# Two decoder layers' attention: pairs of heads across key groups, values in groups, scores at alternate ends of a step

## The chip, the cores and the metric

The kernel runs on one core of a Trainium2 chip. The metric is the device time of one launch in microseconds (us), as the median of a few runs. Smaller is better. All data is 32-bit floating point at input and output.

## The reference, cut to what matters

The reference is one block of a first kind (a mixer, cross attention and a feed-forward net) and then two layers of a second kind, over 512 tokens of width 1024. Only the attention of the two layers of the second kind concerns the change:

```
q, k, v, u, ug, ga, gb = split(rmsnorm(x) @ w_in)          # 16 query heads, 2 key heads, 64 wide
q, k = rope(rmsnorm(q)), rope(rmsnorm(k))
# query block of 128 tokens i sees key blocks i-1 and i; window 128; head n uses key head n // 8
s = q k^T / 8, masked;  m = max(max(s), sink)
p = exp(s - m) / (sum(exp(s - m)) + exp(sink - m));   a = p v
c = conv_branch(u, ug) @ w_conv_out                        # 31 taps, layer norm, silu
x = x + (sigmoid(ga) * a + sigmoid(gb) * c) @ w_out
x = x + feed_forward(x)
```

## The kernel before, in words

Every engine has its own program, written out by hand; semaphores order them, and each engine runs its program strictly in order. Weights come in a stream of units of 1 MB through three slots. ScalarE splits each into a high part (`split_hi`), VectorE takes the rest as a low part (`split_lo`), and each product of a 128x128 weight tile with 512 tokens is three matmuls, high by high, high by low, low by high (lines 415 to 417). Such a triple is called a chunk below.

Inside a layer, the attention is cut into 32 jobs. Job j is one block of 128 queries and one pair of heads. The blocks come in the order 1, 2, 3, 0; a job of block 0 (the last eight, 24 to 31) has one key block instead of two. The stage is a hand-written loop of 36 steps. In step t TensorE does, in this order: the scores of job t (`scores`, line 2110: two heads, each in its own 64 rows of the array), the turning of the probabilities of job t-3 (`turn`, line 2120: up to four 128x128 transposes into one bank), some chunks of other products of the layer that need no attention (`fill_chunks`, counts in `FILL_AT`), and the values of job t-4 (`values`, line 2133: two heads, each in its own 64 columns of the array). Here S(j), T(j) and V(j) name these, and fill(t) the chunks of step t. One fp32 matmul is two records in the trace.

Between them, for each job: VectorE adds the mask and takes the maximum (`softmax`, line 2415, one instruction a head) and, after that of the next job, the reciprocal of the sums (line 2419). ScalarE takes the exponential of both heads (`exps`, line 2260) and copies the turned probabilities to `lprobT` (`copy_turned`, line 2267; there is one bank, so T(j) waits for the copy of j-1). GpSimd scales the probabilities (`scaled`, line 2590). VectorE multiplies the values by the gate (`gated`, line 2427). The three engines do other work of the layer in the same loop: layer norm of the convolution (squares at line 2289, a square root at line 2292, silu at line 2296), gates, weight splits, and from step 29 the merge. A merge of part k is a sum on GpSimd (`merged`, line 2595), its high part on ScalarE (`merged_hi`, line 2273) and its low part on VectorE (`merged_lo`, line 2440). In steps 32 to 35 TensorE takes one part k each, 0 to 3, into the output products (`out_products`, three chunks), and after the loop parts 4 to 7. Each waits for `merged_lo(k)`.

The keys of the two heads of a pair are in one 64-row half of the array; a swapped copy `lkx` of the keys, made by ScalarE, serves the other half.

Of the kernel before, what the change touches and what calls it, by code (L numbers as in the profile page):

```python
# [100 lines left out]
def build(nc, w, x, mem, pos, pack, tables, cmask, w2, wg, rope2, out):  # L101
    ctx = ExitStack()
    with ctx:
# [104 lines left out]
        lkx = place("lkx", [P, T], F32, a)  # L208
# [16 lines left out]
        cos_q, perm_q = place("cos_q", [P, T], F32, a), place("perm_q", [P, P], F32, a)  # L225
        b = [a[0]]
        lsq = place("lsq", [P, 2, T + 4], F32, b)
        lcos = place("lcos", [P, 2, T + 4], F32, b)
        lwide = place("lwide", [P, QB * P], F32, b)
        b = [a[0]]  # L230
        lprob = place("lprob", [P, 4, 2, 2 * P + 2], F32, b)
        lprobT = place("lprobT", [P, 2, 4, P], F32, b)
# [1613 lines left out]
        def cross_dve(dve):  # L1846
# [84 lines left out]
        q_sq, q_ss, q_std, q_inv, q_row, q_n, q_rot, q_cos, q_sin, q_rope, l_kx = (sem("l_" + n) for n in (  # L1931
            "q_sq", "q_ss", "q_std", "q_inv", "q_row", "q_n", "q_rot", "q_cos", "q_sin", "q_rope", "kx"))
# [8 lines left out]
        LJ = QB * 8  # L1941

# [6 lines left out]
        LAG_T, LAG_V = 3, 4  # L1949

# [15 lines left out]
        MERGE_HI_AT, MERGE_LO_AT = 29, 30  # L1966
# [31 lines left out]
        def layer_pe(pe, L):  # L1998
# [99 lines left out]
            def scores(j):  # L2098
                i, tile, g = block_of(j), j % 8, j % 8 // 4
                if j == 0:  # L2100
                    pe.wait_ge(l_kx, L * 2 + 2)
                    pe.wait_ge(l_g, L * 16 + 10)
# [5 lines left out]
                for e in range(2):  # L2108
                    keys = key_rows(lq[:, 8, :], lkx[:, :], e, g)[:, k0:(i + 1) * P]
# [13 lines left out]
            def values(j):  # L2123
                i, g = block_of(j), j % 8 // 4
                first = 1 if i == 0 else 0
                pe.wait_ge(A["turned_copied"], L * LJ + j + 1)
                if j == 0:
                    pe.wait_ge(q_rope, L * 9 + 9)
                else:
                    pe.wait_ge(A["gated"], L * LJ + j)  # L2130
                for c in range(first, 2):
                    for e in range(2):
                        mm = pe.matmul(bank[HD * e:HD * e + HD, 6, 0:P], lv[:, i - 1 + c, g * HD:(g + 1) * HD],  # L2133
                                       lprobT[:, j % 2, 2 * e + c, :], start=(c == first), stop=(c == 1))
# [12 lines left out]
            for t in range(STEPS):  # L2147
                if t < LJ:
                    scores(t)
                if t == 1:  # L2150
                    rotate(8)
                if 0 <= t - LAG_T < LJ:
# [11 lines left out]
                if 0 <= t - LAG_V < LJ:  # L2164
                    values(t - LAG_V)
# [6 lines left out]
                if t == AT_SS:  # L2172
                    pe.wait_ge(ln_add, L * 3 + 3)
                    pe.wait_ge(l_gs, L * 16 + 12)
                    column_sums(pe, bank[:, 7, 0:QB], conv_squares(0)).then_inc(cstat_done, 1)

# [10 lines left out]
        def layer_act(act, L):  # L2187
# [21 lines left out]
            for n in range(V_FILL):  # L2209
# [39 lines left out]
                if n == ROPE_UNITS[0] + 2:  # L2249
                    act.wait_ge(q_rope, L * 9 + 1)  # L2250
# [508 lines left out]
```

## Time and profile before

| what | value |
|---|---|
| median of 3 runs | 2247.55 us (2246.56 to 2248.97) |
| span of the profiled execution | 2246.4 us |
| median less that span | 1.15 us |
| TensorE busy | 2224.9 us, 99% |
| VectorE, ScalarE, GpSimd busy | 1245.1, 885.6, 280.7 us |
| attention stage of layer 0, S(0) to the end of V(31) | 1033.15 to 1154.85 us |

A record of TensorE says when a matmul starts and ends, and the ends are modelled, so its busy share says little about waits. What an operation takes of TensorE's time is read from the start of its first record to the start of the next operation's. Idle time in brackets names the engine that released the instruction. Both layers run the same program; the stage of layer 1 shows the same steps as that of layer 0 to a few hundredths of a microsecond.

### The profile page before, as it was taken

What the parts mean: (1) busy time and instruction counts of PE and PEld (TensorE: products, weight loads), DVE (VectorE), ACT (ScalarE), POOL (GpSimd) and SP (SyncE); (2) the same over time, 40 slices, a digit from 0 to 9 for tenths busy, and PEclk for the clock granted to TensorE, in tenths of its full rate; (3) what the DMA queues carried; (4) which work ended last, traced back from release to release, by engine and by line L of the source; (5) the groups of instructions that cost most, each with busy time, mean ns of one, the idle gap of its engine ahead of it and who ended that gap; (6) DMA issues with size and microseconds to landing.
All of it is one profiled execution on the core that took longest, in us unless ns stands there. A gap on an engine that the chain in (4) does not pass through costs nothing.

```text
span 2246.4 us, 29245 instructions
## 1 busy us (share of the span) xinstructions
PE 2224.9 (99%) x11388; PEld 1821.7 (81%) x11388; DVE 1245.1 (55%) x1836; ACT 885.6 (39%) x1363; POOL 280.7 (12%) x273
## 2 busy tenths in 40 slices
PE   9999999999999999999999999999999999999999
PEld 7877888898888888886778888888887668888887
DVE  6467656445444225999664444333889664544422
ACT  5545454354333225234744333222323753433321
POOL 3000032011000001014331000001003442000000
PEclk9999999999999999999999999999999999999999
DMA  6221033122222231321122222222221112322222
GB/s 223 100 76 57 20 121 126 55 72 99 103 102 93 94 113 69 113 75 57 56 77 81 107 93 93 100 106 105 104 84 57 39 66 85 113 102 104 94 101 86
DMA packets 30484, 203.19 MB, mean 90 GB/s; under 512 B 3504, under 2 KB 4144, under 8 KB 6704
## 3 DMA queue, kind: packets, MB, share of 16 engines
q1 hardware_dynamic: 29088, 197.34, 24.4%
q10 hardware_dynamic: 1296, 4.46, 0.5%
q8 instruction: 69, 1.13, 0.2%
q14 instruction: 31, 0.25, 0.0%
HBM read 199.69 MB, written 2.10 MB: 90 GB/s over the span
## 4 chain that ended last, share of the span: by engine, by line
PE 93%; DVE 3%; POOL 1%; ACT 1%; issue 1%; DMA 0%; ACTq 0%; DVEq 0%; POOLq 0%
PE bank L415 26%; PE bank L417 26%; PE bank L416 26%; PE bank L2110 1%; PE bank L1002 1%; PE bank L2120 1%; PE bank L2133 1%; PE bank L973 1%; PE bank L2028 1%; POOL acc L324 1%; PE bank L990 1%; PE bank L2010 1%; PE bank L1593 1%; PE bank L1570 1%; PE bank L515 1%
## 5 line engine op out<-in xcount | busy, mean ns | idle before, releaser
L415 PE MATMUL bank<-x_hi,w_hi 128*128 128x512 f32 (+1 forms) x2032 | 789.9, 389 | 5.9 <-DVE x_lo L1766 2.3
L417 PE MATMUL bank<-x_hi,w_lo 128*128 128x512 f32 (+1 forms) x2032 | 775.0, 381 | 0.0
L416 PE MATMUL bank<-x_lo,w_hi 128*128 128x512 f32 (+1 forms) x2032 | 774.1, 381 | 0.0
L301 DVE TENSOR_TENSOR w_lo<-w_raw,w_hi 128x2048 fp32r<-128x2048 f32 x167 | 386.2, 2313 | 412.3 <-ACT w_hi L297 412.3
L297 ACT ACTIVATE w_hi<-w_raw 128x2048 fp32r<-128x2048 f32 x167 | 319.7, 1916 | 585.8 <-PE bank L417 583.9
L415 PEld LDWEIGHTS bank<-x_hi,w_hi 128*128 128x128 f32 x2032 | 382.1, 188 | 83.6 <-issue 6.8
L417 PEld LDWEIGHTS bank<-x_hi,w_lo 128*128 128x128 f32 x2032 | 381.9, 188 | 74.9
L416 PEld LDWEIGHTS bank<-x_lo,w_hi 128*128 128x128 f32 x2032 | 382.4, 188 | 72.7 <-issue 2.9
L415 PE MATMUL bank<-f_hi,w_hi 128*128 128x512 f32 (+1 forms) x572 | 213.3, 373 | 0.0
L416 PE MATMUL bank<-f_lo,w_hi 128*128 128x512 f32 (+1 forms) x572 | 213.2, 373 | 0.0
L417 PE MATMUL bank<-f_hi,w_lo 128*128 128x512 f32 (+1 forms) x572 | 213.2, 373 | 0.0
L2345 DVE SCALAR_TENSOR_TENSOR cy<-la,gains,cy 128x512 f32<-128x512 f32 x240 | 173.9, 794 | 0.0
L563 DVE TENSOR_TENSOR bank<-bank,rbc 128x512 f32<-128x512 f32 x66 | 46.0, 697 | 167.6 <-PE bank L417 159.6
L415 PEld LDWEIGHTS bank<-f_hi,w_hi 128*128 128x128 f32 x572 | 107.7, 188 | 19.0
L416 PEld LDWEIGHTS bank<-f_lo,w_hi 128*128 128x128 f32 x572 | 107.7, 188 | 18.9
L417 PEld LDWEIGHTS bank<-f_hi,w_lo 128*128 128x128 f32 x572 | 107.7, 188 | 18.7
L324 POOL TENSOR_TENSOR acc<-acc,sq 128x512 f32<-128x512 f32 (+1 forms) x48 | 77.6, 1618 | 144.2 <-ACT sq L308 140.4
L552 ACT ACTIVATE f_hi<-bank 128x512 f32 x66 | 39.6, 599 | 115.5 <-DVE bank L569 115.5
L571 DVE TENSOR_TENSOR f_lo<-bank,f_hi 128x512 f32 x66 | 45.7, 692 | 58.4 <-ACT f_hi L552 58.4
L2590 POOL TENSOR_TENSOR lprob<-lprob,small 128x512 f32<-128x512 f32 (+1 forms) x64 | 61.9, 967 | 123.6 <-DVE small L2419 77.8
L2260 ACT ACTIVATE lprob<-lprob,small 128x257 f32<-128x257 f32 (+1 forms) x128 | 60.5, 475 | 31.5 <-DVE small L2415 30.9
L324 POOL TENSOR_TENSOR acc<-sq 128x512 f32<-128x512 f32 (+1 forms) x8 | 14.4, 1801 | 442.8 <-ACT sq L308 442.8
(355 smaller groups left out, 2637.2 us busy)
## 6 DMA issues: line engine op xcount, KB each, us to landing
w_raw<-w_d SPq DMA_DIRECT2D x184, 1024.0 KB, 4.8
out_d<-h SPq DMA_DIRECT2D x8, 256.0 KB, 6.6
h<-x_d ACTq DMA_DIRECT2D x3, 512.0 KB, 9.2
tab<-rope_d ACTq DMA_DIRECT2D x2, 640.0 KB, 3.9
memT<-mem_d ACTq DMA_DIRECT2D x1, 1024.0 KB, 4.8
w_raw<-w_d SPq DMA_DIRECT2D x2, 256.0 KB, 4.1
h<-x_d ACTq DMA_DIRECT2D x2, 256.0 KB, 5.8
w_raw<-w_d SPq DMA_DIRECT2D x1, 512.0 KB, 6.6
```

The costliest lines, as they stand in the source:

```text
L297: act.activation(w_hi[:, u.slot, :], w_raw[:, u.slot, :], ACT.Copy).then_inc(hi_ready, 1)
L301: dve.tensor_tensor(w_lo[:, u.slot, :], w_raw[:, u.slot, :], w_hi[:, u.slot, :], ALU.subtract).then_inc(lo_ready, 1)
L324: pool.tensor_tensor(acc[:, 0:width], sq[:, 0, 0:width] if k == 1 else acc[:, 0:width], sq[:, k % 2, 0:width], ALU.add).then_inc(acc_ready, 1)
L415: pe.matmul(dst, wh[:, k, cols], hi[:, kx_, at:at + width], start=start, stop=False)
L416: pe.matmul(dst, wh[:, k, cols], lo[:, kx_, at:at + width], start=False, stop=False)
L417: return pe.matmul(dst, wl[:, k, cols], hi[:, kx_, at:at + width], start=False, stop=stop)
L552: act.activation(pick(f_hi, j, i), up, ACT.Copy).then_inc(f_hi_done, 1)
L563: dve.tensor_tensor(g, g, rbc[:, :], ALU.mult).then_inc(gu_scaled, 1)
L571: dve.tensor_tensor(pick(f_lo, j, i), up, pick(f_hi, j, i), ALU.subtract).then_inc(f_lo_done, 1)
L2260: act.activation(row, row, ACT.Exp, bias=asm(j, 0, e), scale=-1.0, accum_out=asm(j, 4, e)).then_inc(A["exp"], 1)
L2345: dve.scalar_tensor_tensor(out=cy[:, m, :], in0=src, scalar=wt, in1=cy[:, m, :], op0=ALU.mult, op1=ALU.add).then_inc(l_tap, 1)
L2590: pool.tensor_tensor(row, row, asm(j, 12).unsqueeze(2).to_broadcast([P, 2, 2 * P - c0]), ALU.mult).then_inc(A["scaled"], 1)
```

## The change

Heads n and n+8 form a pair, one of each key head, so that each half of the array finds its own key head where the rotated keys lie; `lkx` and its two copies go. The weights' columns are put in that order ahead of the launch. The turned probabilities are kept for four jobs (`lprobT`), and the values of four jobs of one block, or of two in block 0, are one product of up to 512 columns (`GROUPS`, `values(n)`), with one `gated` for the group; they stand in steps 7, 11, 15, 19, 23, 27, 29, 31, 33 and 35. In an even step the scores stand last and not first, and with them that step's `softmax` on VectorE and `exps` on ScalarE: an even job's scores and the next odd job's are then neighbours. The merge starts in step 31 instead of 29 (GpSimd, ScalarE) or 30 (VectorE).

```diff
         a = [scope]
         lq = place("lq", [P, 9, T], F32, a)
-        lkx = place("lkx", [P, T], F32, a)
...
-        cos_q, perm_q = place("cos_q", [P, T], F32, a), place("perm_q", [P, P], F32, a)
+        perm_q = place("perm_q", [P, P], F32, a)
...
+        turned_at = b[0]
         lwide = place("lwide", [P, QB * P], F32, b)
+        cos_q = place("cos_q", [P, T], F32, b)
         b = [a[0]]
         lprob = place("lprob", [P, 4, 2, 2 * P + 2], F32, b)
-        lprobT = place("lprobT", [P, 2, 4, P], F32, b)
+        assert b[0] == turned_at
+        lprobT = place("lprobT", [P, 2, 2, 4, P], F32, b)
...
                                         "pv", "gated")}
         sink_in = sem("a_sink_in")
         LJ = QB * 8
+        GROUPS = [range(j, j + 4) for j in range(0, 24, 4)] + [range(j, j + 2) for j in range(24, LJ, 2)]
+        NG = len(GROUPS)
+        GROUP_OF = [n for n, js in enumerate(GROUPS) for _ in js]
...
         V_FILL = 14
         ROPE_UNITS = range(10, 15)
         LAG_T, LAG_V = 3, 4
+        VALUES_AT = {js[-1] + LAG_V: n for n, js in enumerate(GROUPS)}
+
+        def group_cols(n):
+
+            js = GROUPS[n]
+            return slice(js[0] % 4, js[-1] % 4 + 1)
         FILL_BANK = (5, 7, 5, 7, 7, 5) + (7, 5) * 4
...
         CENTRE_AT, SQ_AT, NORM_AT, LO_AT = ({t: (0, 1), t + 1: (2, 3)} for t in (3, 3, AT_ROWS, AT_LO))
         L_SPLIT_AT = {3: (16, 0), 4: (16, 1), 5: (17, 0), 8: (17, 1), 16: (18, 0), 17: (18, 1), 18: (19, 0), 21: (19, 1),
                       25: (20, 0), 28: (20, 1), 33: (21, 0), 34: (21, 1)}
-        MERGE_HI_AT, MERGE_LO_AT = 29, 30
+        MERGE_HI_AT, MERGE_LO_AT = 31, 31
         OUT_AT = {32: (0,), 33: (1,), 34: (2,), 35: (3,)}
         STEPS = LJ + LAG_V
...
                 if j < 8:
                     pe.wait_ge(q_rope, L * 9 + j + 2)
                     pe.wait_ge(A["max"], (L * LJ + j - 1) * 2)
                 c0, k0 = (P, 0) if i == 0 else (0, (i - 1) * P)
                 for e in range(2):
-                    keys = key_rows(lq[:, 8, :], lkx[:, :], e, g)[:, k0:(i + 1) * P]
+                    keys = lq[HD * e:HD * e + HD, 8, k0:(i + 1) * P]
                     pe.matmul(bank[:, score_bank(j) + e, c0:2 * P], lq[HD * e:HD * e + HD, tile, i * P:(i + 1) * P], keys,
                               start=True, stop=True).then_inc(A["scores"], 1)
...
                         mm = pe.transpose(bank[:, 4, (2 * e + c) * P:(2 * e + c + 1) * P], lprob[:, prob_at(j), e, c * P:(c + 1) * P], ident[:, :])
                 mm.then_inc(A["turned"], 1)
-            def values(j):
-                i, g = block_of(j), j % 8 // 4
+            def values(n):
+                js, cols = GROUPS[n], group_cols(n)
+                i = block_of(js[0])
                 first = 1 if i == 0 else 0
-                pe.wait_ge(A["turned_copied"], L * LJ + j + 1)
-                if j == 0:
+                pe.wait_ge(A["turned_copied"], L * LJ + js[-1] + 1)
+                if n == 0:
                     pe.wait_ge(q_rope, L * 9 + 9)
                 else:
-                    pe.wait_ge(A["gated"], L * LJ + j)
+                    pe.wait_ge(A["gated"], L * NG + n)
                 for c in range(first, 2):
                     for e in range(2):
-                        mm = pe.matmul(bank[HD * e:HD * e + HD, 6, 0:P], lv[:, i - 1 + c, g * HD:(g + 1) * HD],
-                                       lprobT[:, j % 2, 2 * e + c, :], start=(c == first), stop=(c == 1))
+                        mm = pe.matmul(bank[HD * e:HD * e + HD, 6, cols.start * P:cols.stop * P], lv[:, i - 1 + c, e * HD:(e + 1) * HD],
+                                       lprobT[:, e, c, cols, :].rearrange("p m t -> p (m t)"), start=(c == first), stop=(c == 1))
                 mm.then_inc(A["pv"], 1)
...
             fill_chunks(FILL_FIRST)
             for t in range(STEPS):
-                if t < LJ:
+                if t < LJ and t % 2:
                     scores(t)
                 if t == 1:
                     rotate(8)
+                if t in VALUES_AT:
+                    values(VALUES_AT[t])
                 if 0 <= t - LAG_T < LJ:
                     turn(t - LAG_T)
                 fill_chunks(FILL_AT.get(t, 0))
...
                         pe.wait_ge(lo_ready, Unit(base + V_OUT + 1, L).n + 1)
                         pe.wait_ge(co_ready, L * 8 + 8)
                     out_products(((1, 1), (0, 0), (0, 1)), OUT_AT[t])
...
                     pe.wait_ge(ln_add, L * 3 + 3)
                     pe.wait_ge(l_gs, L * 16 + 12)
                     column_sums(pe, bank[:, 7, 0:QB], conv_squares(0)).then_inc(cstat_done, 1)
+                if t < LJ and t % 2 == 0:
+                    scores(t)
             out_products(((1, 1), (0, 0), (0, 1)), range(4, 8)).then_inc(unit_done, 1)
             out_products(((1, 0),), range(8)).then_inc(unit_done, 1)
...
-                    act.activation(lkx[HD:P, :], lq[0:HD, 8, :], ACT.Copy).then_inc(l_kx, 1)
             def exps(j):
...
             def copy_turned(j):
                 act.wait_ge(A["turned"], L * LJ + j + 1)
-                if j >= 2:
-                    act.wait_ge(A["pv"], L * LJ + j - 1)
+                if j == 0:
+                    act.wait_ge(q_rope, L * 9 + 9)
+                if j >= 4:
+                    act.wait_ge(A["pv"], L * NG + GROUP_OF[j - 4] + 1)
                 first = 1 if block_of(j) == 0 else 0
-                act.activation(lprobT[:, j % 2, :, :].rearrange("p (e c) t -> p e c t", e=2)[:, :, first:, :],
+                act.activation(lprobT[:, :, first:, j % 4, :],
                                bank[:, 4, :].rearrange("p (e c t) -> p e c t", e=2, c=2)[:, :, first:, :], ACT.Copy)\
                    .then_inc(A["turned_copied"], 1)
...
             for t in range(STEPS):
                 if 0 <= t - LAG_T < LJ:
                     copy_turned(t - LAG_T)
-                if t < LJ:
+                if t < LJ and t % 2:
                     exps(t)
                 for f in FILL_END.get(t - 1, ()):
                     if f < 6:
                     for m in range(4):
                         act.wait_ge(ln_y, L * 4 + m + 1)
                         act.activation(c_hi[:, m, :], cy[:, m, :], ACT.Copy).then_inc(ln_hi, 1)
+                if t < LJ and t % 2 == 0:
+                    exps(t)
                 if MERGE_HI_AT <= t:
                     merged_hi(t - MERGE_HI_AT)
...
                     dve.wait_ge(A["exp"], (L * LJ + o + 1) * 2)
                     dve.reciprocal(asm(o, 12), asm(o, 4)).then_inc(A["rec"], 1)
-            def gated(j):
-                i, tile = block_of(j), j % 8
-                dst = sga[:, tile, i * P:(i + 1) * P]
-                dve.wait_ge(A["pv"], L * LJ + j + 1)
-                if j == 0:
+            def gated(n):
+                js, cols = GROUPS[n], group_cols(n)
+                i, tile = block_of(js[0]), js[0] % 8
+                dst = sga[:, tile:tile + len(js), i * P:(i + 1) * P]
+                dve.wait_ge(A["pv"], L * NG + n + 1)
+                if n == 0:
                     dve.wait_ge(l_g, L * 16 + 8)
-                dve.scalar_tensor_tensor(out=dst, in0=dst, scalar=1.0, in1=bank[:, 6, 0:P], op0=ALU.add, op1=ALU.mult).then_inc(A["gated"], 1)
+                pv = bank[:, 6, cols.start * P:cols.stop * P].rearrange("p (m t) -> p m t", t=P)
+                dve.scalar_tensor_tensor(out=dst, in0=dst, scalar=1.0, in1=pv, op0=ALU.add, op1=ALU.mult).then_inc(A["gated"], 1)
             def conv_gated(k):
...
             taps(FIRST_TAPS)
             for t in range(STEPS):
-                softmax(t, t - 1)
-                if 0 <= t - LAG_V < LJ:
-                    gated(t - LAG_V)
+                if t % 2 or t >= LJ:
+                    softmax(t, t - 1)
+                if t in VALUES_AT:
+                    gated(VALUES_AT[t])
                 if t == STEPS - 1:
-                    dve.wait_ge(A["gated"], L * LJ + LJ)
+                    dve.wait_ge(A["gated"], L * NG + NG)
...
                 for m in LO_AT.get(t, ()):
                     dve.wait_ge(ln_hi, L * 4 + m + 1)
                     dve.tensor_tensor(c_lo[:, m, :], cy[:, m, :], c_hi[:, m, :], ALU.subtract).then_inc(ln_lo, 1)
+                if t % 2 == 0 and t < LJ:
+                    softmax(t, t - 1)
             for k in range(STEPS - MERGE_LO_AT, DT):
                 merged_lo(k)
...
                 pool.tensor_tensor(row, row, asm(j, 12).unsqueeze(2).to_broadcast([P, 2, 2 * P - c0]), ALU.mult).then_inc(A["scaled"], 1)
             def merged(L, k):
-                pool.wait_ge(A["gated"], L * LJ + 3 * 8 + k + 1)
+                pool.wait_ge(A["gated"], L * NG + GROUP_OF[24 + k] + 1)
                 pool.wait_ge(co_ready, L * 8 + k + 1)
                 pool.tensor_tensor(sgb[:, k, :], sgb[:, k, :], sga[:, k, :], ALU.add).then_inc(mg_sum, 1)
                         sums_of_squares(L, (0,) if j == 6 else (1, 2))
                     if j > 0:
                         scaled(L, j - 1)
-                    if j > 28:
-                        merged(L, j - 29)
-                for k in range(LJ - 28, DT - 1):
+                    if j >= LJ - 1:
+                        merged(L, j - LJ + 1)
+                for k in range(2, DT - 1):
                     merged(L, k)
                 for n in (1, 2) if L + 1 < LAYERS else (1,):
                     sum_squares(pool, L * 2 + NORM_L + n)
...
     stream += bg[:1] + spans(g["w1_kc"], 0, 256) + bg[1:] + spans(g["w1_vc"], 0, 256) + cg + xin
     stream += spans(g["w_out"], 0, D) + spans(g["w_kv_x"], 0, 2 * D) + spans(g["w_q_x"], 0, D) + spans(g["w_o_x"], 0, D)
     stream += ffn_units(g["w_gate_up"], g["w_down"])
+    paired = np.concatenate([np.r_[HD * t:HD * t + HD, HD * (8 + t):HD * (8 + t) + HD] for t in range(8)])
+    sink_order = np.arange(16).reshape(2, 8).T.reshape(-1)
...
```

## Rows read from the trace of the kernel before

**Rows 1.** Page: busy time of each engine; granted clock in 40 slices.

```profile
...
PE 2224.9 (99%) x11388; PEld 1821.7 (81%) x11388; DVE 1245.1 (55%) x1836; ACT 885.6 (39%) x1363; POOL 280.7 (12%) x273
...
PEclk9999999999999999999999999999999999999999
```

**Rows 2.** Timeline of TensorE, layer 0: start, us, engine, line, operation.

```profile
...
1073.10 0.65 PE L2120 MATMUL bank<-ident,lprob 128*128 128x128 f32 x4
1073.69 0.66 PE L2133 MATMUL bank<-lprobT,lv 128*64 128x128 f32 x8
1074.28 0.48 PE L2110 MATMUL bank<-lkx,lq 64*128 64x256 f32 x1
...
1074.91 0.66 PE L2120 MATMUL bank<-ident,lprob 128*128 128x128 f32 x4
1075.32 0.48 PE L415 MATMUL bank<-x_hi,w_hi 128*128 128x512 f32 x1
...
1076.10 0.39 PE L415 MATMUL bank<-x_hi,w_hi 128*128 128x512 f32 x1
...
1076.78 0.39 PE L415 MATMUL bank<-x_hi,w_hi 128*128 128x512 f32 x1
...
1077.55 0.66 PE L2133 MATMUL bank<-lprobT,lv 128*64 128x128 f32 x8
```

**Rows 3.** Timeline of TensorE: first two score jobs, and the column sums.

```profile
...
1033.15 0.45 PE L2110 MATMUL bank<-lq 64*128 64x256 f32 x1 [0.70 <-issue]
...
1034.22 1.12 PE L2028 MATMUL bank<-lq,perm_q 128*128 128x512 f32 x2
...
1043.48 3.70 PE L2170 MATMUL bank<-cy,ones 128*128 128x512 f32 x8
```

**Rows 4.** Timeline of TensorE, step 5 of layer 0: the turns.

```profile
...
1050.53 0.63 PE L2120 MATMUL bank<-ident,lprob 128*128 128x128 f32 x4 [0.91 <-ACT lprobT L2267]
```

**Rows 5.** Timeline of ScalarE, steps 7 to 9 of layer 0.

```profile
...
1064.83 0.60 ACT L2267 ACTIVATE lprobT<-bank 128x512 f32<-128x512 f32 x1 [0.27 <-PE bank L2120]
1065.44 1.28 ACT L2260 ACT_TABLE_LOAD   x1
1066.74 0.51 ACT L2260 ACTIVATE lprob<-lprob,small 128x257 f32<-128x257 f32 x1
...
1067.65 0.19 ACT L2260 ACTIVATION_READ_ACCUMULATOR lprob<-lprob,small 128x1 f32 x1
...
1069.21 0.57 ACT L2267 ACTIVATE lprobT<-bank 128x512 f32<-128x512 f32 x1
```

**Rows 6.** Timeline of VectorE and ScalarE in the stretch of rows 2.

```profile
...
1073.80 0.60 ACT L2267 ACTIVATE lprobT<-bank 128x512 f32<-128x512 f32 x1 [1.34 <-PE bank L2120]
...
1075.12 0.55 DVE L2415 CUSTOM_DVE_ANT_0 lprob<-bank,mask_b,neg_sink 128x256 f32<-128x256 f32 x1 [0.44 <-PE bank L2110]
```

**Rows 7.** Groups by line, 1033 to 1160 us: busy, mean ns, idle.

```profile
...
L2595 POOL TENSOR_TENSOR sgb<-sgb,sga 128x512 f32<-128x512 f32 x7 | 10.7, 1529 | 2.0 <-DVE sga L2427 2.0
...
L2440 DVE SCALAR_TENSOR_TENSOR o_lo<-sgb,o_hi 128x512 fp32r<-128x512 f32 x8 | 6.7, 853 | 0.0
...
L2273 ACT ACTIVATE o_hi<-sgb 128x512 fp32r<-128x512 f32 x8 | 5.0, 630 | 9.3 <-POOL sgb L2595 8.0 <-DVE sgb L2452 1.4
```

**Rows 8.** Timeline, last steps of layer 0's attention, four engines.

```profile
...
1132.18 0.41 DVE L2415 CUSTOM_DVE_ANT_0 lprob<-bank,mask_b,neg_sink 128x128 f32<-128x128 f32 x1 [0.23 <-PE bank L2110]
...
1132.72 0.40 ACT L2260 ACTIVATE lprob<-lprob,small 128x129 f32<-128x129 f32 x1
...
1132.85 0.16 DVE L2419 RECIPROCAL small<-small 128x2 f32<-128x2 f32 x1
...
1133.15 0.61 POOL L2590 TENSOR_TENSOR lprob<-lprob,small 128x256 f32<-128x256 f32 x1 [1.21 <-DVE small L2419]
...
1143.77 0.41 PE L2120 MATMUL bank<-ident,lprob 128*128 128x128 f32 x2 [1.29 <-ACT lprobT L2267]
...
1154.85 0.50 PE L415 MATMUL bank<-o_hi,w_hi 128*128 128x512 f32 x1
```

More of the change, by code:

```diff
@@ L1930, in build @@
             "u", "ug_scaled", "sigmoid", "a", "tap", "q", "v_raw", "v_turned", "v"))
-        q_sq, q_ss, q_std, q_inv, q_row, q_n, q_rot, q_cos, q_sin, q_rope, l_kx = (sem("l_" + n) for n in (
-            "q_sq", "q_ss", "q_std", "q_inv", "q_row", "q_n", "q_rot", "q_cos", "q_sin", "q_rope", "kx"))
+        q_sq, q_ss, q_std, q_inv, q_row, q_n, q_rot, q_cos, q_sin, q_rope = (sem("l_" + n) for n in (
+            "q_sq", "q_ss", "q_std", "q_inv", "q_row", "q_n", "q_rot", "q_cos", "q_sin", "q_rope"))
         l_gs, l_g = sem("l_gates_scaled"), sem("l_gates")
@@ L2098, in scores @@
             def scores(j):
-                i, tile, g = block_of(j), j % 8, j % 8 // 4
+                i, tile = block_of(j), j % 8
                 if j == 0:
-                    pe.wait_ge(l_kx, L * 2 + 2)
                     pe.wait_ge(l_g, L * 16 + 10)
@@ L2163, in layer_pe @@
                     out_products(((1, 1), (0, 0), (0, 1)), OUT_AT[t])
-                if 0 <= t - LAG_V < LJ:
-                    values(t - LAG_V)
                 if t == AT_SUM:
@@ L2248, in layer_act @@
                     act.activation(perm_q[:, :], perm2, ACT.Copy, scale=col("q_norm", 0, L)).then_inc(q_tabs, 1)
-                if n == ROPE_UNITS[0] + 2:
-                    act.wait_ge(q_rope, L * 9 + 1)
-                    act.activation(lkx[0:HD, :], lq[HD:P, 8, :], ACT.Copy).then_inc(l_kx, 1)
-                    act.activation(lkx[HD:P, :], lq[0:HD, 8, :], ACT.Copy).then_inc(l_kx, 1)
             def exps(j):
@@ L2444, in layer_dve @@
             for t in range(STEPS):
-                softmax(t, t - 1)
-                if 0 <= t - LAG_V < LJ:
-                    gated(t - LAG_V)
+                if t % 2 or t >= LJ:
+                    softmax(t, t - 1)
+                if t in VALUES_AT:
+                    gated(VALUES_AT[t])
                 if t == STEPS - 1:
-                    dve.wait_ge(A["gated"], L * LJ + LJ)
+                    dve.wait_ge(A["gated"], L * NG + NG)
                     dve.wait_ge(mg_sum, L * 8 + 7)
@@ L2704 @@
             stream += spans(wl, u + half, u + half + 256) + spans(wl, ug + half, ug + half + 256)
-        stream += spans(wl, q, q + 1024) + spans(wl, kv, kv + 256)
-        stream += spans(wl, ga, ga + 2048) + spans(g["w_conv_out_2"][l], 0, D, rows=4) + spans(g["w_out_2"][l], 0, D)
+        stream += spans(wl, 0, 0, order=q + paired) + spans(wl, kv, kv + 256)
+        stream += spans(wl, 0, 0, order=np.r_[ga + paired, ga + D + paired])
+        stream += spans(g["w_conv_out_2"][l], 0, 0, rows=4, order=paired) + spans(g["w_out_2"][l][paired], 0, D)
         stream += ffn_units(g["w_gate_up_2"][l], g["w_down_2"][l])
@@ L2721 @@
         cols += [tiles(g["norm_mix_2"][l]), tiles(g["norm_ffn_2"][l]), np.tile(g["q_norm_2"][l], 2)[:, None],
-                 np.tile(g["k_norm_2"][l], 2)[:, None], np.broadcast_to(g["sinks_2"][l], (P, 16)),
+                 np.tile(g["k_norm_2"][l], 2)[:, None], np.broadcast_to(g["sinks_2"][l][sink_order], (P, 16)),
                  g["conv_w_2"][l].reshape(TAPS, 4, P).transpose(2, 1, 0).reshape(P, 4 * TAPS), tiles(g["conv_b_2"][l]),
```

## The prediction

> **What bounds the kernel now.** I read the page first: TensorE is busy 99% of the span, the next engine 55%, at the full clock in every slice [rows 1]. So only what TensorE is spared, or made to wait, moves the end. Its ends are modelled, so I then read the timeline of TensorE by starts. Two steps of layer 0, one with no chunk and one with three, read so [rows 2]: T takes 0.59 if V follows (1073.10 to 1073.69), V 0.59, S 0.63 (1074.28 to 1074.91), T 0.41 if chunks follow, three chunks 2.23. The reader is to see that nothing waits here, and yet the same operation has two prices, by what comes next: T followed by chunks, both 128x128, is 0.18 cheaper than T followed by V, which uses 64 columns. Two score jobs side by side took 1.07 together (1033.15 to 1034.22, [rows 3]) against 2 x 0.63, so each is 0.44 and 0.19 is paid once. A chunk is 0.68 (1076.10 to 1076.78), so three are 2.04, and again 0.19 is left ahead of V. So a change of the array's shape costs 0.19, and pure times are S 0.44, T 0.41, V 0.40. Last I read the waits: before T(2) 0.91 [rows 4], before T(29) 1.29 [rows 8], and little between.
>
> **What it removes: changes of shape.** From the program's order I count where neighbours on TensorE differ among 64-row (S), 64-column (V) and 128x128 (T, chunks): 100 a layer before, 44 after, as an odd step's scores follow the even step's at once, and ten V stand where there were 32. Of the 56 saved, 13 lie ahead of the end of S(9), and 43 behind it: 13 x 0.19 = 2.5 and 43 x 0.19 = 8.2 us a layer.
>
> **Values as one product.** A group of four is eight records of 512 columns, two halves of the array at a time, so four in a row. The nearest row of such a length is the column sums, eight records of 512 columns one after another in 3.63 (1043.48 to 1047.11), 0.45 each [rows 3]; four are 1.75 with a little less at the end. Four V now are 4 x 0.40 = 1.6. So I add 0.15 a group and 0.07 a pair: +1.0 us from group 1 on. Bounds: 0 if a column costs what it costs now, and +1.75 a group more if the halves don't overlap at this length; that they overlap at 128 columns is seen in V's 0.40 for eight records, against 0.41 for four turns of the same length [rows 2]. I take the first kind of price.
>
> The Trainium skill (TensorEngine Tiling (Array Packing), section Performance Considerations) states some 60 cycles of overhead for each matmul, so that fewer and longer ones gain. By it I estimate 24 records saved a group at 25 ns, two at a time: 0.3 a group, 3.6 us in the launch, in place of my 2 us more: a sum of +3.8 and not of +9.4. The rows speak against it here: records of 128 columns take 0.10 and those of 512 take 0.45, so there is no fixed part to save.
>
> **Edits that cost nothing.** The two copies to `lkx` go from ScalarE ahead of the stage, where S(0) waits for gates and not for them. One `gated` for four jobs spares VectorE starts; it is not what V waits for in steps four apart. The weights are as many bytes in another order. No DMA is added or moved past a queue.
>
> **What it adds: waits for ScalarE's queue.** T(j) waits for the copy of j-1 out of the one bank. A copy starts 0.70 after its turn starts (1073.10 to 1073.80) and takes 0.60 [rows 2, 6]. So two T with nothing between leave 1.35, of which T itself is 0.41: a wait of 0.95. Before, V and S always lay between. Now an odd step's T and the next even step's T have only the odd step's chunks between. Besides, ScalarE's order in an even step is now copy, other work, exponentials, so the next copy stands behind the even job's exponentials. With S(even) at 0: maximum at 0.85 (1074.28 to 1075.12, [rows 2, 6]), exponentials about 0.6 later (0.54 for a short job, [rows 8]), lasting 1.10 (1066.74 to 1067.84, [rows 5]), then the copy of 0.60 and a hand-over: the next T at 3.25. Without V in the odd step TensorE is ready at 0.88 + 0.19 + 0.41 + 0.68n = 1.48 + 0.68n for n chunks.
>
> Steps 0 to 8, walked through like this: the convolution's taps on VectorE, then layer norm's squares on ScalarE ahead of the copy of job 1, end the waits of T(1) to T(3). That chain hardly changes: T(2) started at 1050.53 after 0.91 for the copy [rows 4], and my walk puts it at 1050.8. The 2.5 us of spared changes are idle there. I book nothing: 0.
>
> From step 9 on, per layer. T(7): ScalarE runs one line from copy to copy, 1064.83, table load 1.28, exponentials, a gate, a split, copy at 1069.21, that is 4.38 [rows 5]. Before, TensorE had T(6), chunks, V(5) and S(10) to do meanwhile, and hardly waited. Now S(10) and V come later, and there are T(6) and three chunks. In my walk the square root ahead of that line waits for TensorE's sums, which stand behind the first group of V: copy 5 is at 65.2, copy 6 at 69.75, T(7) at 70.35, and TensorE is ready at 68.3: +2.0. T(9): no chunk in step 11, V ahead of T(8): +0.95. T(11): n = 0 and a spread of four blocks, as long as a turn, ready at 1.9 against 3.25: +1.3. T(19) and T(23): n = 2, ready at 2.85: +0.4 and, with a short job, +0.25. The group of step 27, behind a split on ScalarE: +0.55. Together 5.4. Bounds: 2.2, if only the uncovered T(9) and T(11) stand, and 7.
>
> **The merge, moved to step 31.** This is the largest term. In GpSimd's queue `merged(0)` now stands behind `scaled(30)`, which needs the reciprocal that VectorE issues after the maximum of job 31. With S(30) at 0: maxima of 30 from 0.63 (0.85 less the shorter scores), with its reciprocal 0.67 + 0.16 later at 1.45 [rows 8], the same for 31: reciprocal 30 at 2.25. Scaling 0.30 later, 0.61 long [rows 8]: 3.15. Merge 1.53, high part 0.63, low part 0.68 at best (0.85 mean) [rows 7], hand-overs 0.2: product part 0 can start at 6.2. TensorE has S(30), S(31), a pair of V, T(28), one chunk, T(29) (which waits 0.4 for the copy behind the exponentials): ready at 2.75. Wait 3.45. Part 1 again: `scaled(31)` stands behind the reciprocal that VectorE issues after `merged_lo(0)`, at 6.35; merge, high, low end at 10.1, TensorE at 9.3: 0.85. Parts 2 and 3: 0.2. Then step 35: the last pair's gate, `merged(6)`, the sum of part 7 on VectorE, and only behind it in VectorE's order `merged_lo(4)`. The gate waits for a split (16.7), so 0.4 + 1.7 + 0.7 + 0.7 with hand-overs: 20.4; TensorE has done part 3 at 17.5: 2.9. Sum with T(29): 7.8, against 1.36 before at T(29) (1.29 in its row, [rows 8]), when out(4) followed V(31) at 1154.85 without a wait. So +6.4. Bounds: +4, if the last three operations meet idle engines (1.7 in place of 2.9, and a shorter merge), and +8.
>
> Sum per layer: -8.2 + 1.0 + 5.4 + 6.4 = +4.6; a walk of all times, by which S(30) falls level with before and part 4 starts late by all that follows, gives +5.05. I take +4.7, both layers +9.4. Against the profiled execution, 2246.4 + 9.4 = 2255.8 span; the median of the runs lies 1.15 above that span, so 2257.
>
> **Rivals.** 0.2%, 4.5 us, is about what a measurement tells from no change. The tail is hidden: the later merge costs no more than T(29) did, because TensorE comes late enough. For it: the merge's mean times hold other queues' stalls. Against: the order of GpSimd's and VectorE's programs. 9.4 - 2 x 6.4 = -3.4: 2244, no change. 0.15.
>
> The other side, faster: ScalarE's copies of steps 2 to 12 come in time. Then the head's 2.5 and the 4.2 of T(7), T(9) and T(11) are kept in each layer: 9.4 - 13.4 = -4; it is decided at a copy that ends within 1.0 us of its turn where no chunk lies between. For it: ScalarE is busy 39% [rows 1]. Against: the table load in its line, and T(2)'s wait before [rows 4, 5]. 2243, the edge of faster. 0.10.
>
> The halves don't overlap at 512 columns: 6 x 1.75 + 4 x 0.4 = 12 a layer, +24: 2281. 0.04. Or each record has a fixed part. If that were a quarter of a short record's 0.10, a group would take 1.2 + 0.1 in place of 1.75, 2.8 less a layer with the pairs: 9.4 - 5.6 = 3.8: 2251, no change. Against: 0.45 for 512 columns [rows 3]. 0.05. It is the reading of the Trainium skill cited above.
>
> TensorE's clock falls. The largest wait of the stage before, 1.29 [rows 8], left the grant at full speed [rows 1]; one of 3.45 is not in this stage. If the next part's 2.05 us ran at half speed, 1.2 GHz, it would be 2 more for each long wait, 4 to 8 in all: 2261 to 2265. 0.10. The Trainium skill (TensorE: Matmul & The Clock Gate, Part 1) says that an idle engine is put at the lower level; by it 2261 or more, and the waits of this trace don't show it.
>
> **How the numbers follow.** The forecast has 0.56: 2257, its own range 2252 to 2262: 2.5 a layer either way, about half of what the lower bounds of the merge (2.4 less) and of the copies (3.2 less) allow together. The range 2244 to 2263 takes in the hidden tail, the fixed part and half of the clock; the others, under 0.2, stay out. Faster: 0.10, the other side. Same: 0.20, the hidden tail and the fixed part. Slower: 0.70.
>
> **What would show it.** Right: V to S to T replaced by two S at 1.07 with no gap, V groups near 1.75, TensorE idle before T(7), T(9), T(11), released by the copies, and before the first and the fifth output part, released by `merged_lo`, near 3.4 and 2.9. Level times at S(30). Wrong: a tail without those two waits, or ScalarE's copies ahead of the turns, and I am too high; a granted clock under 1.0, or groups of 3.4, and I am too low.

## The result, and the profile after

| | median | lowest to highest | runs | span of the profiled execution |
|---|---|---|---|---|
| before | 2248.41 us | 2246.56 to 2249.52 | 5 | 2246.4 us |
| after | 2256.85 us | 2255.27 to 2259.13 | 5 | 2254.8 us |

The ratio is 1.0038, 95% interval 1.0027 to 1.0049: slower by 0.4%, 8.4 us in span and in median. The forecast was 2257, 9.4 more.

The page of the kernel after, busy time and granted clock:

```profile
PE 2213.7 (98%) x11068; PEld 1810.5 (80%) x11068; DVE 1235.7 (55%) x1792; ACT 880.2 (39%) x1359; POOL 273.5 (12%) x273
...
PEclk9999999999999999999999999999999999999999
```

Against [rows 1] TensorE has 11.2 us less to do (2224.9 to 2213.7). Outside its work stand 2246.4 - 2224.9 = 21.5 us before and 41.1 after: 19.6 more. The change does spare TensorE work, and more than all of it is lost to waiting. What does it wait for, in the whole launch (total, times, longest)? Before, one wait of these kinds was above 0.5 us in total,

```profile
PE bank L2120 <- ACT lprobT L2267: 4.4, 4, 1.3
```

and after there are five:

```profile
PE bank L417 <- DVE o_lo L2455: 9.8, 6, 2.9
PE bank L2130 <- ACT lprobT L2278: 7.0, 4, 2.1
PE bank L2130 <- POOL lprob L2608: 4.5, 6, 1.1
...
PE bank L2144 <- ACT lprobT L2278: 1.5, 4, 0.5
PE bank L335 <- POOL la L2622: 1.6, 2, 0.8
```

Line numbers have moved: 417 is the chunk (415 before), 2120 the scores, 2130 the turn, 2144 the values, 2278 `copy_turned`, 2608 `scaled`, 2613 `merged`, 2284 `merged_hi`, 2455 `merged_lo`. The first row is the late merge, the next two the turns. The timeline of TensorE in steps 0 to 14 of layer 0, which answers to [rows 2 to 4]:

```profile
1032.67 1.14 PE L2120 MATMUL bank<-lq 64*128 64x256 f32 x8 [0.66 <-ACT sgb L2214]
1033.73 1.13 PE L2039 MATMUL bank<-lq,perm_q 128*128 128x512 f32 x2
...
1050.37 0.63 PE L2130 MATMUL bank<-ident,lprob 128*128 128x128 f32 x4 [2.10 <-ACT lprobT L2278]
...
1058.22 1.94 PE L2144 MATMUL bank<-lprobT,lv 128*64 128x512 f32 x8
1060.09 0.66 PE L2130 MATMUL bank<-ident,lprob 128*128 128x128 f32 x4
...
1069.61 0.63 PE L2130 MATMUL bank<-ident,lprob 128*128 128x128 f32 x4 [1.40 <-ACT lprobT L2278]
...
1074.48 0.66 PE L2130 MATMUL bank<-ident,lprob 128*128 128x128 f32 x4
...
1075.92 0.63 PE L2130 MATMUL bank<-ident,lprob 128*128 128x128 f32 x4 [0.78 <-POOL lprob L2608]
...
1080.12 0.60 PE L342 MATMUL bank<-ident,rcol_ln 128*128 128x128 f32 x4
1081.77 0.63 PE L2130 MATMUL bank<-ident,lprob 128*128 128x128 f32 x4 [1.06 <-POOL lprob L2608]
```

Two jobs' scores take 1.06 to the next start, as forecast. A group of four values takes 1.87 (1058.22 to 1060.09), or 1.68 without its change of shape: the halves overlap at 512 columns. T(2), T(7), T(9) and T(11) wait. For T(9) and T(11) the profile names GpSimd, where the forecast named ScalarE. The timeline of all engines there, with the scalings counted from job 0, says otherwise for T(9) and shows a tie for T(11):

```profile
1073.63 1.04 POOL L2608 TENSOR_TENSOR lprob<-lprob,small 128x512 f32<-128x512 f32 x1 [2.29 <-ACT lprob L2269]
...
1075.18 0.60 ACT L2278 ACTIVATE lprobT<-bank 128x512 f32<-128x512 f32 x1 [1.04 <-PE bank L2130]
...
1080.64 1.04 POOL L2608 TENSOR_TENSOR lprob<-lprob,small 128x512 f32<-128x512 f32 x1 [4.72 <-ACT lprob L2269]
1081.05 0.58 ACT L2278 ACTIVATE lprobT<-bank 128x512 f32<-128x512 f32 x1
```

The scaled job 9 is there at 1074.67 and the copy of job 8 only at 1075.78: T(9) waits for the copy, as forecast. (The profile names GpSimd probably because the scaling of job 10 ends at the same moment, 1075.79.) The scaled job 11 is there at 1081.68 and the copy of job 10 at 1081.63: at T(11) either alone would hold the turn as long. The end of the stage, which answers to [rows 8], in the timeline of all engines:

```profile
1141.31 0.41 PE L2130 MATMUL bank<-ident,lprob 128*128 128x128 f32 x2
...
1141.82 1.26 POOL L2613 TENSOR_TENSOR sgb<-sgb,sga 128x512 f32<-128x512 f32 x1
...
1143.11 0.63 ACT L2284 ACTIVATE o_hi<-sgb 128x512 fp32r<-128x512 f32 x1 [0.97 <-POOL sgb L2613]
...
1143.77 0.69 DVE L2455 SCALAR_TENSOR_TENSOR o_lo<-sgb,o_hi 128x512 fp32r<-128x512 f32 x1 [1.76 <-ACT o_hi L2284]
...
1144.61 0.60 PE L417 MATMUL bank<-o_hi,w_hi 128*128 128x512 f32 x1 [2.89 <-DVE o_lo L2455]
...
1145.86 0.63 PE L417 MATMUL bank<-o_hi,w_hi 128*128 128x512 f32 x1
...
1148.42 0.65 PE L2144 MATMUL bank<-lprobT,lv 128*64 128x256 f32 x4
...
1152.75 0.50 PE L417 MATMUL bank<-o_hi,w_hi 128*128 128x512 f32 x1 [1.01 <-DVE o_lo L2455]
...
1158.96 0.50 PE L417 MATMUL bank<-o_hi,w_hi 128*128 128x512 f32 x1 [1.01 <-DVE o_lo L2455]
```

Read it from the bottom of the chain up: out(0) waits for `merged_lo(0)`, that for `merged_hi(0)`, that for `merged(0)`, which starts when `scaled(30)` has left GpSimd. Then the chunks of out(0) start some 1.26 apart instead of 0.68. The windows of that stretch show why (length, busy time of TensorE, its weight loads, VectorE, ScalarE, GpSimd, each with its number of records, then TensorE's granted clock):

```profile
1138.00:1142.00 4.00, 3.65 (x24) 2.00 (x22) 2.99 (x13) 1.89 (x9) 1.50 (x4) 1.00 0.54 176
1142.00:1146.00 4.00, 1.39 (x4) 1.13 (x5) 0.78 (x3) 1.04 (x4) 2.39 (x3) 0.85 0.21 86
1146.00:1150.00 4.00, 4.00 (x17) 2.60 (x16) 1.50 (x2) 1.16 (x3) 3.82 (x4) 0.72 0.00 0
```

The grant was at 1.2 GHz for part of two windows, behind the wait; the page's 40 slices of 56 us don't show it. Layer 1 has the same (0.89 and 0.68 from 1838 to 1846).

### The profile page after: what moved, and what is told of

Its sections match the earlier page's. It is cut to its first block, busy times and chain, and to the rows that moved or that the text cites. A ratio compares the mean times of both kernels' runs of the same rounds, so it can differ in the third digit from the quotient of the medians.

```text
span 2254.8 us, 28511 instructions
## 1 busy us (share of the span) xinstructions
PE 2213.7 (98%) x11068; PEld 1810.5 (80%) x11068; DVE 1235.7 (55%) x1792; ACT 880.2 (39%) x1359; POOL 273.5 (12%) x273
## 4 chain that ended last, share of the span: by engine, by line
PE 85%; DVE 7%; POOL 2%; issue 2%; ACT 2%; DMA 0%; ACTq 0%; DVEq 0%; POOLq 0%
PE bank L417 25%; PE bank L419 24%; PE bank L418 24%; DVE cy L2358 3%; PE bank L1004 1%; DVE w_lo L303 1%; PE bank L2130 1%; PE bank L975 1%; PE bank L2144 1%; POOL sgb L2613 1%; POOL acc L326 1%; PE bank L992 1%; POOL lprob L2608 1%; PE bank L2120 1%; PE bank L2021 1%
## 5 line engine op out<-in xcount | busy, mean ns | idle before, releaser
L419 PEld LDWEIGHTS bank<-f_hi,w_lo 128*128 128x128 f32 x572 | 107.7, 188 | 18.8
L2428 DVE CUSTOM_DVE_ANT_0 lprob<-bank,mask_b,neg_sink 128x256 f32<-128x256 f32 (+1 forms) x128 | 59.6, 504 | 31.0 <-PE bank L2120 30.9
```

The source lines that it names most:

```text
L419: return pe.matmul(dst, wl[:, k, cols], hi[:, kx_, at:at + width], start=False, stop=stop)
L2428: dve.tensor_tensor_reduce(lprob[:, prob_at(j), e, c0:2 * P], bank[:, score_bank(j) + e, c0:2 * P], mask_b[:, c0:2 * P], query_factor(j, e ...
```

## The experiments

The theory was the forecast's: the spared changes of shape are real, and they are paid away at two places, the turns that wait for ScalarE's copies in steps 2 to 12, and the output parts that wait for the late merge. Rivals: the values' wider product or the new order of a step costs it, or the clock that falls.

**The merge back in steps 29 and 30**, the rest of the change kept.

```diff
-        MERGE_HI_AT, MERGE_LO_AT = 31, 31
+        MERGE_HI_AT, MERGE_LO_AT = 29, 30
...
-                    if j >= LJ - 1:
-                        merged(L, j - LJ + 1)
-                for k in range(2, DT - 1):
+                    if j > 28:
+                        merged(L, j - 29)
+                for k in range(4, DT - 1):
```

> The changed kernel with one part undone: the merge starts in step 29 (GpSimd, ScalarE) and 30 (VectorE) again, all else as changed. Theory A (the tail waits because the merge's queue positions are late): walking the queues, T(29) waits about 2.3 for the copy behind the second high part, but out(0), out(2) and out(4) wait for nothing, so the tail gives back some 4.8 us a layer: about 2247, that is level with the kernel before (within 3 us). Rival B (TensorE arrives at the tail too early whatever the merge's place, and the step order is what costs): the wait only moves, at most 2 us come back: 2254 or more.

Measured: 2248.38, ratio to before 1.0000 (0.9991 to 1.0009), 8.5 us under the kernel after. No wait for `o_lo` is left; what is left, over layer 0's stage, is led by

```profile
PE bank L2130 <- ACT lprobT L2278: 5.7, 3, 2.2
PE bank L2130 <- POOL lprob L2608: 2.2, 3, 1.1
```

So the whole loss against before is the late merge's, with what follows it, and everything else in the change nets to nothing. The third wait in the first row is at T(29): 2.16, for the copy of job 28, which ScalarE starts at 1143.30 behind `merged_hi(1)`, itself waiting for GpSimd.

**The other way round: the kernel before, with only the merge late.**

```diff
-        MERGE_HI_AT, MERGE_LO_AT = 29, 30
+        MERGE_HI_AT, MERGE_LO_AT = 31, 31
...
-                    if j > 28:
-                        merged(L, j - 29)
-                for k in range(LJ - 28, DT - 1):
+                    if j >= LJ - 1:
+                        merged(L, j - LJ + 1)
+                for k in range(2, DT - 1):
```

> The kernel before with one part of the change alone: the merge starts in step 31 on all three engines; scores, pairs and values as before. Theory A (the late merge by itself makes TensorE wait): T(29)'s 1.36 goes, out(0) waits some 3 and out(4) 1 to 3, with a slow stretch behind the long wait: 4 to 5 us a layer, 2256 to 2259. Rival (in the kernel before TensorE comes late enough, so that the late merge is hidden): 2247 to 2251.

Measured: 2268.93 (2262.55 to 2269.22), ratio 1.0089 (1.0075 to 1.0103). The sign is as expected, and the size expected was far too low. The profiled execution is its quickest run, 2262.55, span 2260.5; there the waits and the windows are

```profile
PE bank L415 <- DVE o_lo L2440: 6.6, 5, 2.7
...
1144.00:1148.00 4.00, 3.36 (x9) 2.67 (x9) 0.57 (x2) 0.68 (x2) 3.28 (x4) 0.57 0.00 0
```

Five waits a layer instead of three, and the clock falls too (0.57). By that execution the late merge costs 14 us in the kernel before. The median lies 6 above it: three of the five runs have a mean granted clock of 0.994 (0.998 in the profiled one). They left no trace, so where they lose it stays open.

**TensorE kept busy through the wait before out(0)**, by 13 products of ones into a spare bank.

```diff
+                        keep_running(pe, 13)
                     out_products(((1, 1), (0, 0), (0, 1)), OUT_AT[t])
```

> The changed kernel with 13 extra 128x128 products of constants into an unused bank ahead of the first output part, so that TensorE is busy for most of its 2.9 us wait there; they are work that nothing uses. Theory A (the long wait lets the clock fall to 1.2 GHz, and the slow stretch behind it is a cost of its own): granted clock 1.00 in the tail, out(0) back to 2.05 from 3.6, the wait itself unchanged: 1.5 us a layer less, about 2254. Rival (the slow records are caused by the merge's engines sharing memory with TensorE's reads, and the clock is only a sign): records of out(0) stay near 0.42, 2257 within 1, or 2258 if the extra products come in the way.

Measured: 2255.87 (2254.28 to 2257.31), ratio 1.0034 (1.0021 to 1.0047). TensorE's timeline at out(0), and the windows of the same stretch:

```profile
1143.98 0.48 PE L417 MATMUL bank<-o_hi,w_hi 128*128 128x512 f32 x1
...
1146.23 0.65 PE L2144 MATMUL bank<-lprobT,lv 128*64 128x256 f32 x4
```

```profile
1142.00:1146.00 4.00, 4.00 (x29) 3.57 (x28) 0.77 (x2) 1.38 (x3) 2.39 (x4) 1.00 0.00 0
1146.00:1150.00 4.00, 3.80 (x19) 2.29 (x17) 2.24 (x3) 2.09 (x5) 4.00 (x4) 1.00 0.00 0
```

The grant stays at 2.4 GHz and out(0) takes 2.25 instead of 3.81, with the data no earlier. So the 1.56 is the clock's. From S(30) to VectorE's first sum of the residual it saves 1.1 in layer 0 (28.59 to 27.46): the 13 products end after the data are there, so that out(0) starts 6.18 behind S(30) and not 5.74, and 0.44 is lost again. In layer 1 the grant stayed at 1.00 here as well, but fell at another place, behind T(2)'s wait. In the median, 1.0 below the kernel after, it isn't resolved. The clock is a real term, but a small one.

**Scores first in every step**, the old order, with pairs, groups and late merge kept.

```diff
-                if t < LJ and t % 2:
+                if t < LJ:
                     scores(t)
...
-                if t < LJ and t % 2 == 0:
-                    scores(t)
```

and likewise `exps` and `softmax`.

> The changed kernel with the opposite order undone: scores, maximum and exponentials stand first in every step again; pairs across key groups, grouped values and the late merge stay. Theory A: 30 more changes of shape a layer (5.7 us at 0.19) against ScalarE waits before turns that mostly go (T(2), T(7), T(9), T(11): some 5 us), and the tail's wait stays: 2254 to 2260, near the changed kernel. Rival B (scores last is what made it slower): near the kernel before or under it, 2246 to 2250.

Measured: 2254.73 (2252.17 to 2256.30), ratio 1.0028 (1.0018 to 1.0038). There are 74 changes of shape a layer in place of 44, and yet it is 2.1 faster than the change. Its waits in layer 0's stage:

```profile
PE bank L417 <- DVE o_lo L2451: 4.8, 4, 2.6
PE bank L2130 <- ACT lprobT L2276: 2.7, 3, 1.5
```

The turns' waits fall from 5.8 (3.5 + 2.3, below) to 2.7. So the alternating order spares 30 changes a layer and loses at least as much. The rows show half of that coming back at the turns; that it is the exponentials between two copies, and the missing cover between two turns, is read from the order of the programs. How much each spared change was worth at its place was not taken apart. A part of the 2.1 is the clock: behind out(0)'s wait of 2.56 the grant stayed at 1.00 in layer 0, and fell behind the same wait in layer 1 (0.86 and 0.72 from 1836 to 1844). But in layer 1, with the fall, the stage is still 1.2 shorter than the change's (125.11 and 126.27, in the table below).

**Values job by job**, with the order and the late merge of the change.

```diff
-        GROUPS = [range(j, j + 4) for j in range(0, 24, 4)] + [range(j, j + 2) for j in range(24, LJ, 2)]
+        GROUPS = [range(j, j + 1) for j in range(LJ)]
```

> The changed kernel with groups of one job: values of each job are a product of 128 columns again, one gate a job; pairs across key groups, opposite order and late merge stay. Theory A (a change of shape costs 0.19, a product of 512 columns costs about four of 128): some 36 more changes of shape a layer, 6.8 us, less 1.0 for shorter values: 5 to 6 a layer, 2266 to 2269. Rival C (grouped values are what costs, by their length or by the longer wait for the last copy of a group): 2257 or less.

Measured: 2261.94 (2258.67 to 2263.25), ratio 1.0058 (1.0046 to 1.0071): 5.1 above the change, not 9 or more. It has 82 changes a layer, 38 more, 7.2 us a layer by the price of 0.19, of which a third shows. The turns' waits that the change has are nearly gone in layer 0:

```profile
PE bank L417 <- DVE o_lo L2455: 2.9, 3, 2.4
PE bank L2144 <- DVE sga L2442: 2.2, 3, 1.3
PE bank L335 <- POOL la L2622: 2.1, 1, 2.1
PE bank L2144 <- ACT lprobT L2278: 1.3, 1, 1.3
...
PE bank L2130 <- POOL lprob L2608: 0.4, 1, 0.4
```

The turns' 5.8 became 0.4: V between them is cover for the copies. But much of it comes back elsewhere, as 3.5 ahead of the values (0.7 in the change) and 2.1 ahead of the sums in step 7 (0.8). In all, the stage waits 9.6 instead of 12.9, and that 3.3 is the part that the expectation left out. The clock muddies the size: in this execution the grant also falls behind the wait of 2.1, and for longer behind out(0)'s (0.94, 0.50 and 0.71 from 1144 to 1156). Even so the rival that the grouped values are the loss falls: among runs with a mean granted clock of 0.998, job by job takes 2258.67 and 2261.11, the change 2255.27 to 2256.85.

**Chunks moved to where the turns are uncovered**, late merge kept: in each of steps 10, 12 and 14 two chunks that stood behind the turn go to the step before, and so ahead of T(7), T(9) and T(11).

```diff
-        FILL_AT = {1: 6, 2: 2, 3: 1, 5: 4, 6: 4, 7: 2, 9: 3, 10: 2, 12: 3, 14: 6,
+        FILL_AT = {1: 6, 2: 2, 3: 1, 5: 4, 6: 4, 7: 2, 9: 5, 11: 2, 12: 1, 13: 2, 14: 4,
```

> The changed kernel with the same chunks placed otherwise: two of step 10 go to step 9, two of step 12 to step 11, two of step 14 to step 13, so that each of the turns T(7), T(9) and T(11) has two chunks more ahead of it. Theory A (those three turns wait 1.5, 1.0 and 1.1 us for the copy before them because nothing lies between): the three waits go, 3.6 us a layer, 2249 to 2251. Rival (ScalarE's queue is the bound of the stretch, so that the wait only moves to the next turn or group): 2254 or more.

Measured: 2250.23 (2249.12 to 2251.79), ratio 1.0009 (1.0000 to 1.0018), 6.6 below the change. The turns' waits in layer 0's stage, first the change, then this kernel (the merge's rows are the same in both, 4.9):

```profile
PE bank L2130 <- ACT lprobT L2278: 3.5, 2, 2.1
PE bank L2130 <- POOL lprob L2608: 2.3, 3, 1.1
```

```profile
PE bank L2130 <- ACT lprobT L2278: 2.1, 1, 2.1
...
PE bank L2130 <- POOL lprob L2608: 0.4, 1, 0.4
```

Of 5.8 at the turns 2.5 is left, T(2) above all, and 2 x 3.3 is the 6.6. The same chunks at other steps, and nothing else: so those waits were TensorE with nothing to do, not a longer operation.

**Both**: the chunks moved, and the merge early, but with `merged_hi(1)` in step 31, behind the copy of job 28 that it had held up. The chunks' diff is that of the last experiment, GpSimd's that of the first; VectorE's loop goes by `LO_AT_` as ScalarE's by `HI_AT`; the rest is

```diff
-        MERGE_HI_AT, MERGE_LO_AT = 31, 31
+        HI_AT = {29: (0,), 31: (1,), 32: (2,), 33: (3,), 34: (4, 5)}
+        LO_AT_ = {30: (0,), 32: (1,), 33: (2, 3), 34: (4, 5)}
...
-                if MERGE_HI_AT <= t:
-                    merged_hi(t - MERGE_HI_AT)
+                for k in HI_AT.get(t, ()):
+                    merged_hi(k)
```

> The placing of chunks as in the run beside it, and the merge early again, but with its high parts kept out of the way of the copies: part 0 in step 29, 1 in 31, 2 in 32, 3 in 33, 4 and 5 in 34 (low parts in 30, 32, 33, 33, 34, 34). Theory A: the tail's waits go (4.2 a layer by the run with the early merge), T(29)'s 2.1 behind the second high part too, and the 3.6 of the three turns: 2237 within 3, under both kernels. Rival (either part's wait comes back elsewhere in the queue): 2243 or more.

Measured: **2238.06** (2235.47 to 2239.24), ratio 0.9959 (0.9945 to 0.9972): faster than both kernels, 10.3 under before and 18.8 under the change. Its page, the longest of its waits in layer 0's stage, and TensorE's timeline at the end of it:

```profile
PE 2208.4 (99%) x11068; PEld 1808.4 (81%) x11068; DVE 1238.2 (55%) x1792; ACT 880.5 (39%) x1359; POOL 275.2 (12%) x273
```

```profile
PE bank L2131 <- ACT lprobT L2279: 2.1, 1, 2.1
```

```profile
1136.14 0.41 PE L2131 MATMUL bank<-ident,lprob 128*128 128x128 f32 x2
1136.94 0.47 PE L417 MATMUL bank<-o_hi,w_hi 128*128 128x512 f32 x1 [0.39 <-issue]
```

T(29) and out(0) wait about 0.8 together, by their starts; T(2)'s wait of 2.1 is still there. TensorE's work is 16.5 under before. Of it 12.9 reaches the end in this execution, the quickest of five (span 2233.5), and 10.3 in the median.

**All kernels by the stage alone.** A median holds the whole launch, and the grant falls at other places of it too. The stage itself, from the start of S(0) to the start of out(4) (before, in layer 0, 1154.85 - 1033.15), read from the timelines of TensorE in both layers, and the places in it where windows of 4 us show a grant under 1.00:

| kernel | layer 0 | layer 1 | the grant falls behind the wait of |
|---|---|---|---|
| before | 121.70 | 121.72 | none |
| after | 126.29 | 126.27 | out(0), both layers |
| merge early | 121.21 | 122.60 | T(2), layer 1 |
| kept busy | 125.12 | 126.46 | T(2), layer 1 |
| scores first | 123.98 | 125.11 | out(0), layer 1 |
| values job by job | 129.76 | 129.44 | the sums and out(0), both layers |
| chunks moved | 122.72 | 122.71 | out(0), both layers |
| both | 116.23 | 116.24 | none |
| late merge alone | 129.26 | 129.39 | out(0), both layers |

Where the clock does the same in both layers, the two agree within 0.02 in four of six kernels (0.13 and 0.32 in the others). One fall moves the stage by 1.1 to 1.4 (merge early, kept busy, scores first, between their layers). So the effects of the first two and the last two experiments are beyond what the clock or chance moves. No run takes back the pairs across key groups by themselves.

## Why the prediction was right

The time forecast, 2257, and the time measured, 2256.85, agree better than the working does. The forecast's sum was 9.4 and the measured difference is 8.4. The rest is luck: the 1.15 that it added to the span set a median against the span of another run; the profiled run after takes 2256.85 and has a span of 2254.8, 2.05 less.

By place, per layer; measured in layer 0 from starts in the timelines, the forecast from its own terms (its 43 changes and two pairs split at out(0)):

| place | forecast | measured |
|---|---|---|
| S(0) to out(0), the wait ahead of out(0) (before: of T(29)) left out | -1.2 | -0.6 |
| T(29) and out(0): less the 1.36 before | +2.5 | +1.7 |
| out(0) at the lower clock | 0 | +1.6 |
| out(1) | +0.85 | 0 |
| parts 2 and 3 | +0.2 | +1.2 |
| out(4) | +2.9 | +1.3 |
| changes of shape behind out(0) | -0.6 | -0.8 |
| sum | +4.6 | +4.4 |

By the table above the stage is 4.6 longer in either layer, so the rows leave 0.2 of it unplaced. Twice 4.6 is 9.2, and the span grew by 8.4: outside the stages the launch is 0.7 shorter, 0.5 of it ahead of S(0) of layer 0. That is chance, as this S(0) starts anywhere from 1031.09 to 1034.79 in the nine executions. How the measured ones are worked out: S(0) to out(0) without its wait is 1141.51 - 1032.67 = 108.84 after and 1142.58 - 1033.15 = 109.43 before, with the same operations done. The 1142.58 is the start of V(27) in TensorE's timeline before,

```profile
1142.04 0.44 PE L2133 MATMUL bank<-lprobT,lv 128*64 128x128 f32 x4
```

with 0.37 for V and 0.17 for T(29). A wait is the start of the next operation less the pure time of the one before (1144.61 - 1141.31 - 0.2 = 3.1 at out(0), with two short transposes at 0.2).

- **Changes of shape** at 0.19: right. Pairs of scores stand 1.06 from start to next, with no gap.
- **The group of values**: 1.68 against 1.75. The forecast's own choice held, and so the rival of halves that don't overlap and that of a fixed part in each record both fall: with a quarter of a short record fixed it would be 1.3. The Trainium skill (TensorEngine Tiling (Array Packing), Performance Considerations) gives some 60 cycles of overhead for each matmul; these rows don't show them: eight records of 128 columns take 0.40 and eight of 512 take 1.68, 4.2 times as long.
- **The turns**: T(7) 1.5 (forecast 2.0), T(9) 1.0 (0.95), T(11) 1.1 (1.3), T(19) 0.3 (0.4). The step that names ScalarE's copy as the one releaser holds but for T(11), where GpSimd's scaling ends within 0.05 of the copy. It is late because VectorE issues the reciprocal of job 11 behind the maximum of job 12, whose scores now stand last in step 12 (1078.56): a second wait in the same place that the forecast didn't name. Moving the chunks covers both.
- **The head, booked at nothing**: T(2) waits 2.1 against 0.91 in [rows 4] and starts at 1050.37 (the walk's 1050.8). Ahead of the sums in step 7 the wait for GpSimd's squares grew from 0.26 to 0.78, which wasn't foreseen.
- **The merge**: the mechanism was right, and it is the whole loss (the first experiment). Out(0) was forecast to wait 3.45 and waits 3.1. What failed is what follows it. The clock, a rival at 0.10 that I didn't put in the sum, fell for out(0) and cost 1.6. I had read the grant from slices of 56 us [rows 1], which can't show such a fall; windows of 4 us have the stage before at 1.00 throughout, but 0.96 and 0.61 from 220 to 228, where no wait of TensorE is above 0.63. And out(4) was mis-sized: it waits 1.3 and not 2.9. That isn't the clock's doing, for in the kernel kept busy, where the grant stayed up, out(4) still waits 1.4: there the chain to part 4 ends 19.0 behind S(30), and not 20.4 as forecast, while TensorE is ready at 17.5, as forecast. The late out(0) does explain out(1), which waits 0.3 in the kernel kept busy and not at all after. The total came out near the forecast partly because these errors have opposite signs.
- **The tail hidden**, and **ScalarE in time**: both fall. The waits are there.

Where the gain went: into two new groups of waits, for the merge and at the turns. Undoing the first gives 8.5 us, covering the second 6.6, both, with the order of ScalarE mended, 18.8.

## What to carry to other kernels

Operations that spare time when they are put side by side were also the cover of what stood between them: before neighbours are joined, look at what the engine behind each of them needs from one to the next (here a copy, and once a scaling: 1.44 from T(8) to T(9), of which the turn is 0.41), and bring other work in between. A chain over three engines (sum, high part, low part) that feeds the bound engine must start a full chain's length ahead of its use; two steps later cost 8.5 us here, all that the change lost. When a change moves little, subtract the busy time from the span before and after: here 11.2 us less work and 19.6 us more idle time said at once that it was worth mending.

## What the runs showed of the hardware

- Behind a wait of 2.9 us TensorE's grant fell to 1.2 GHz (window means of 0.85 and 0.72) and the next three chunks started some 1.26 apart instead of 0.68. Kept busy through that wait it stayed at 2.4 GHz, in both layers. So a long pause can cost twice: itself, and what follows it at the lower clock. The Trainium skill (TensorE: Matmul & The Clock Gate, Part 1) says that an idle engine goes to the lower level; here that held behind out(0)'s wait of 2.9 in both layers.
- The length of the wait alone doesn't decide it. In one execution (scores first) the same wait of 2.56 left the grant at 1.00 in layer 0 and was followed by 0.86 and 0.72 in layer 1; T(2)'s wait of 2.1 was followed by a fall in layer 1 of two kernels and in no other stage that has it; and from 220 to 228 the kernel before fell to 0.61 with no wait above 0.63 near it. One fall in the stage cost 1.1 to 1.4 of its length.
- Runs of one kernel differ with the mean granted clock: before, those at 1.000 have spans of 2244.5 to 2246.1, those at 0.998 2246.6 to 2247.9. So a part of the spread that looks like noise goes with the clock.
- In a launch of 2250 us, chunks moved between neighbouring steps, with no instruction added or removed, were worth 6.6 us.
